# A page loop on TensorE: the first score quarter and the third page quarter take an earlier place

## The reference, cut to what matters

```python
def mla_sample_attend(qn, qr, c_kv, k_r, p, ckv_pool, kr_pool, page_table):
    ckv_past = ckv_pool[page_table].reshape(Bsz, -1, KV_RANK).astype(c_kv.dtype)
    kr_past = kr_pool[page_table].reshape(Bsz, -1, B_ROPE).astype(k_r.dtype)
    q_lat = jnp.einsum('bthd,rhd->bthr', qn, p['w_uk'])
    s_past = (jnp.einsum('bthr,bsr->bhts', q_lat, ckv_past)
              + jnp.einsum('bthe,bse->bhts', qr, kr_past)).astype(F32) * ATTN_SCALE
    ...
    w = jax.nn.softmax(jnp.concatenate([s_past, s_new], axis=-1), axis=-1).astype(c_kv.dtype)
    o_lat = (jnp.einsum('bhts,bsr->bthr', w[..., :n_past], ckv_past)
             + jnp.einsum('bhts,bsr->bthr', w[..., n_past:], c_kv))
```

## Time and profile before

| | |
|---|---|
| median of the runs | 3398.93 us (3389.02 to 3408.89) |
| profiled execution | 3408.58 us, its span 3406.4 us |
| PE busy | 3222.7 us (95%) |
| DVE, ACT, POOL busy | 1360.0 us, 1061.2 us, 133.6 us |
| granted TensorE clock, mean | 0.964 of full speed |
| the two page loops | from 885.9 to 1048.7 us and from 2558.4 to 2721.3 us of the span |

### The profile page before, as it was taken

How to read it: one execution, slowest core, us unless ns; L and a number is a source line. 1 busy time by engine, 2 the same in 40 slices (tenths; PEclk the granted TensorE clock), 3 DMA queues, 4 the chain that set the end, 5 groups by cost and what they waited for, 6 DMA issues and landing times.

```text
span 3406.4 us, 68469 instructions
## 1 busy us (share of the span) xinstructions
PE 3222.7 (95%) x27800; PEld 3014.7 (89%) x27800; DVE 1360.0 (40%) x1874; ACT 1061.2 (31%) x1555; POOL 133.6 (4%) x168
## 2 busy tenths in 40 slices
PE   8999999989998999999999999999899999899997
PEld 7999989767777998999999999987677789899996
DVE  3333345366333454333333334444653334533334
ACT  3222134134343323222232222331534433222213
POOL 0000000000330000000000000000013200000000
PEclk9999999689998999999999999997999989999999
DMA  5332321021561332232232222301125423232321
GB/s 133 90 89 79 84 72 47 1 62 36 207 237 49 89 93 68 86 88 85 63 101 86 85 85 63 94 23 45 22 100 221 162 74 96 63 88 87 89 86 55
DMA packets 443324, 296.49 MB, mean 87 GB/s; under 512 B 24327, under 2 KB 430571, under 8 KB 434985
## 3 DMA queue, kind: packets, MB, share of 16 engines
q1 hardware_dynamic: 430265, 217.05, 22.7%
q0 software_dynamic: 12928, 77.64, 6.1%
HBM read 286.44 MB, written 8.34 MB: 87 GB/s over the span
## 4 chain that ended last, share of the span: by engine, by line
PE 88%; DVE 5%; ACT 4%; issue 2%; DMA 0%; ACTq 0%; SPq 0%; DVEq 0%
PE ps L636 66%; PE ps L971 3%; PE ps L986 2%; PE ps L664 2%; PE ps L1007 2%; PE ps L676 1%; PE ps L917 1%; DVE x_lo L1554 1%; PE ps L989 1%; PE ps L908 1%; PE ps L755 1%; PE ps L895 1%; ACT prob L1367 1%; DVE att_nm L1747 1%; PE ps L1023 1%
## 5 line engine op out<-in xcount | busy, mean ns | idle before, releaser
L1502 DVE TENSOR_TENSOR w_lo<-w_raw,w_hi 128x1024 fp32r<-128x1024 f32 x436 | 533.5, 1225 | 1032.4 <-ACT w_hi L1171 1027.8
L636 PE MATMUL ps<-x_hi,w_hi 128*128 128x268 f32 x4032 | 839.7, 290 | 26.1 <-DVE x_lo L1554 17.7
L1171 ACT ACTIVATE w_hi<-w_raw 128x1024 fp32r<-128x1024 f32 x436 | 460.8, 1058 | 1188.6 <-PE ps L636 1175.8
L636 PE MATMUL ps<-x_lo,w_hi 128*128 128x268 f32 x4032 | 830.4, 287 | 0.0
L636 PE MATMUL ps<-x_hi,w_lo 128*128 128x268 f32 x4032 | 829.0, 287 | 0.0
L636 PEld LDWEIGHTS ps<-x_hi,w_hi 128*128 128x128 f32 x4032 | 632.1, 189 | 34.1 <-DVE x_lo L1554 24.7
L636 PEld LDWEIGHTS ps<-x_lo,w_hi 128*128 128x128 f32 x4032 | 634.6, 190 | 0.0
L636 PEld LDWEIGHTS ps<-x_hi,w_lo 128*128 128x128 f32 x4032 | 631.5, 189 | 0.0
L636 PE MATMUL ps<-h_hi,w_hi 128*128 128x268 f32 x1408 | 289.9, 288 | 5.0 <-issue 2.8
L636 PE MATMUL ps<-h_hi,w_lo 128*128 128x268 f32 x1408 | 290.8, 288 | 0.0
L636 PE MATMUL ps<-h_lo,w_hi 128*128 128x268 f32 x1408 | 289.4, 287 | 0.0
(11 more groups left out here) (369 smaller groups left out, 3667.5 us busy)
## 6 DMA issues: line engine op xcount, KB each, us to landing
w_raw<-in_ffn_up SPq DMA_DIRECT2D x180, 512.0 KB, 3.8
w_raw<-in_w_in SPq DMA_DIRECT2D x72, 512.0 KB, 3.9
w_raw<-in_ffn_down SPq DMA_DIRECT2D x64, 512.0 KB, 3.8
w_raw<-in_ffn_down SPq DMA_DIRECT2D x32, 384.0 KB, 3.3
w_raw<-in_w_o SPq DMA_DIRECT2D x16, 512.0 KB, 3.8
c_smp<-in_state_C SPq DMA_DIRECT2D x16, 256.0 KB, 3.0
out_new_C_sample<-c_smp SPq DMA_DIRECT2D x16, 256.0 KB, 2.4
w_raw<-in_w_pa SPq DMA_DIRECT2D x16, 256.0 KB, 2.8
```

The lines of the kernel that those rows point to most:

```text
L636: ins = mm(ps[0:m, 2 * p + half, 0:HT], w[:, s, off + t_ * m:off + t_ * m + m], x[part][:, k0 + t_, half * HT:(half + 1) * HT], start=firs ...
L1171: f(w_hi[:, s, :], w_raw[:, s, :], ACT.Copy).then_inc(hi_made, 1)
L1502: v.tensor_tensor(w_lo[:, s, :], w_raw[:, s, :], w_hi[:, s, :].bitcast(F32), ALU.subtract).then_inc(lo_made, 1)
```

## The change

Two pieces of PE's list change place in each unit that has an old unit. The first score quarter now stands ahead of the old unit's turned probabilities, and the third page quarter ahead of the old unit's values. ACT's list follows: the third quarter's left half is copied before the old unit's values are read out. DVE, POOL and the DMA queues keep their lists.

```diff
@@ PE, in sequence() @@
                                 turn_q(l, i, h2, 0, b)
                                 turn_q(l, i, h2, 1, b)
+                                score_q(l, i, h2, 0)
                                 if before:
                                     turn_p(n - 1)
-                                score_q(l, i, h2, 0)
+                                turn_q(l, i, h2, 2, b)
                                 if before:
                                     values_p(n - 1, (b - 1) % PAGE_BUFFERS)
-                        turn_q(l, i, h2, 2, b)
                         score_q(l, i, h2, 1)
@@ ACT, in sequence() @@
                                     read_p(n - 1)
+                                left_half(l, i, h2, 2)
+                                if before:
                                     read_o(n - 1, i - 1 + h2, 1 - h2)
-                        left_half(l, i, h2, 2)
                         left_half(l, i, h2, 3)
```

## The result

The changed kernel took 3445.28 us (median of six runs, 3434.29 to 3456.35) against 3399.51 us before; the ratio is 1.012 with a 95% interval of 1.0089 to 1.015. It is slower, as forecast, but by 45.8 us between the medians and not by 19. Two later comparisons gave 1.0123 (1.0077 to 1.017) and 1.0103 (1.0072 to 1.0134). Three later executions, one of the changed kernel (4022 us) and two of the kernel before (4519 and 10815 us), lie far outside of all others and are left out everywhere.

What follows compares the result with a forecast made beforehand. PE was taken to bound the kernel, busy 3222.7 of 3406.4 us. Per unit 0.61 + 0.03 = 0.64 us, times 30 units 19.2 us, on the median 3398.93 gave 3418 us; range 3396 to 3436.

Steps and rivals of the forecast that it cites:

- The first scores gain nothing.: Start of each unit: the first scores wait for ACT's copy, so moving turn_p away gains 0 us.
- turn_p falls on the full part of the list, with two more changes of width.: PE, first to second scores: 4.37 us instead of 3.76, 0.61 more, 0.44 of it for the transposes.
- p_t is just covered.: Ahead of the old values: turn_p and third quarter fill 1.40 us, so p_t is there 0.06 us early.
- The added register operation.: Between ACT's copy and the first scores: 0.1 us on top in half of the units, taken as 0.03 a unit.
- Outside of the 30 units nothing changes: Rest of the kernel: no cost; in a layer's first unit the third quarter only changes place with two rotary transposes.
- a lower clock I leave out: Page loop: the hole grows to some 1 us in 10.9, taken not to lower the clock; no cost counted.
- sooner scores: Rival, first scores: turn_p holds them, gain up to 0.92 us; 3390 us, or 3403 for half; chance 0.19 together.
- a full drain at each change of width: Rival, TensorE: each added change costs 0.27 us, 30 us in all, 3429 us; chance 0.13 together with late p_t.
- a later p_t: Rival, old values: p_t starts 0.3 us later, 0.24 more a unit, 3425 us; chance 0.13 together with full drain.
- theory P: From the follow-up runs, not the forecast: where stages behind the loop fall in time decides how long they run at half clock.

Runs made afterwards that it cites:

- e2: Kernel before with only the first score quarter moved ahead of the old probabilities, third page quarter in its old place: period 11.87 us, mean span 3455.7 us.
- e4: Kernel before with ACT copying the next unit's first rotary rows ahead of the exponential: period 9.99 us, ratio 1.0011 to the kernel before.
- e8: Changed kernel with ACT copying the next unit's first rotary rows ahead of the exponential: period 10.71 us, mean span 3417.6 us.
- e3: Kernel before with only the third page quarter moved ahead of the old values, ACT's left half following: period 10.53 us, mean span 3424.9 us.
- e1: Changed kernel run again, unaltered, against the kernel before: ratio 1.0123, period 10.98 us.
- e11: Changed kernel run again, unaltered, in turn with its version with 22 added products, on one chip: 3430.6 us.
- padded version: Changed kernel with 22 products on constants on PE behind each layer's page loop: 3425.8 us against 3430.6 unpadded, side by side.
- e5: Kernel before with 102 products on constants on PE behind each layer's page loop: mean span 3425.9 us, 239 us at half clock.

## Why the prediction was right in the loop and wrong in the time

*The first scores gain nothing.* Right: 2.86 against 2.87 us after the maximum, and 2.80 against 2.71 in every second unit; e2, e4 and e8 show that ACT's chain sets their start.

*turn_p falls on the full part of the list, with two more changes of width.* Right, a little short: 0.72 us from first to second scores instead of 0.61. The 0.11 lie in turn_p to third quarter (0.49 for 0.44) and rotary rows to scores (0.37 for 0.31): both are steps out of a short piece, and took some 0.05 more than their products. The whole period grew by 0.73 us (0.64 forecast), 22 us for 30 units (19.2). The steps are those of one unit; the period is a mean over both kinds.

*p_t is just covered.* Right: there 0.17 us early; e2 shows the wait it would have been, 0.69 us.

*The added register operation.* About right. It was to come on top in every second unit, with 0.1 us, and there the scores start 0.09 later (2.80 against 2.71), some 0.045 a unit where 0.03 stood in the sum. e2, which has it too, also shows 2.80, and e3, which has not, 2.71. No run takes the operation out alone.

*"Outside of the 30 units nothing changes", and "a lower clock I leave out".* These are the steps that failed. I asked only whether the hole would lower the clock inside the loop; it didn't (0.99 in both). But the stages outside of it run partly at half clock, for how long differs from run to run, and each us there costs about 0.42. In the first six runs the changed kernel stood 289 us at half clock, against 233 in all runs of the kernel before: 56 x 0.42 = 23 us, which with 19 at equal half-clock time makes 42, and their mean span, 3443.2 us, lies 41 above the mean of before. Over all its 17 runs it is 37 us more, and 31 and 29 us in the two sets of runs that it shares with the kernel before (e1, e11). So about 12 to 15 us of time go with this kernel, and some 8 to 11 were the draw of those six runs. I also took the spread of three runs for noise that a median wears down to 8 us; it is these same half-clock times, and in both shared sets the changed kernel's were the longer.

The rivals: sooner scores are refuted (e2), a full drain at each change of width is refuted as to size (e3), and a later p_t did not occur.

What makes the changed kernel stand longer at half clock stays open. The profiles show where a part of it lies. Behind the loop one piece answers to the list: in both layers of all six profiles of the changed kernel, of its padded version and of the third quarter alone, the last values run at a clock of 0.57 to 0.60 over 3.3 us, and in the other eight profiles at 1.00. That is 1.0 to 1.3 us a layer, 2.1 to 2.4 in all, and the padded version has it too. The larger part lies elsewhere. Of the 37.6 us between the two profiled spans (3444.0 - 3406.4) the loops have 22 and the stretch ahead of them 13.0; in the three profiles of the changed kernel that stretch took 898.9, 876.5 and 873.6 us. No edit to the loop can shift what runs ahead of it. So theory P can at best explain what happens behind the loop, and the pads do not show even that. The half-clock time rose for all four kernels of e1 to e4, on one chip, and for none of e5 to e8, on another, so the chip or the set of runs is a rival to the order of the list; that the changed kernel stood 29 us higher on a third chip (e11) speaks against the chip alone. How an edit to the loop could act on the stretch ahead, or whether those runs met it by chance, no run tells.

## What to carry to other kernels

Work that stands in a hole is free only there: before moving it, look at what ends the hole, and if that is another engine's chain, shorten the chain or put more into the hole rather than take something out. Where an engine's clock has two levels, an edit of 20 us can come out as one of 40 through stages that it doesn't touch; compare the runs' granted clocks first, fit the spans by them, and read the edit's own price from its period in the trace. Before a difference is put down to an edit, look how much of it lies ahead of the edit, and whether the runs were made side by side.

## What the runs showed of the hardware that I had not expected

Spans of 187 runs of 11 kernels follow a constant plus 0.42 us for each us at half clock, to within 1.6 us. The same program ahead of the loop took 865.9 to 898.9 us, at granted clocks of 0.97 to 0.93. The values behind the loop take 3.27 us in place of 1.93 where the clock falls during them. And a change between full-width transposes and 32-column products cost 0.10 to 0.15 us on TensorE, with the next product starting before the modelled end of the last one.
